# Moving the S5 branch of a two-block network kernel in beside the retention products

## What is computed

```python
def even_mixer(h, pos, w_in, w_out, ...):
    proj = h @ w_in                      # (512, 1024) @ (1024, 2560)
    q, k, v, g, u = jnp.split(proj, [512, 1024, 1536, 2048], axis=-1)
    ret = retention(rotary(heads(q), pos), rotary(heads(k), pos), heads(v))
    ret = head_layer_norm(ret).transpose(0, 2, 1, 3).reshape(bsz, s_len, RET_WIDTH)
    ret = silu(g) * ret
    ssm = s5_mixer(u, ...)
    return jnp.concatenate([ret, ssm], axis=-1) @ w_out

def s5_mixer(u, ...):
    # x_t = a * x_{t-1} + B u_t, complex, 32 groups of 16 channels with 64 states
    _, states = lax.associative_scan(combine, (a, bu), axis=1)
    y = jnp.einsum('gcp,bsgp->bsgc', c_mat, states).real + d_skip * uf
    y = gelu(y)
    return y * sigmoid(y @ w_glu)
```

## Time and profile before

| | |
|---|---|
| median of 3 runs | 3015.39 us (3014.43 to 3018.1) |
| the profiled execution, its own time | 3018.45 us |
| its span | 3016.6 us |
| TensorE busy | 2796.2 us, 93% of the span |
| VectorE busy | 1603.4 us, 53% |
| ScalarE busy | 1150.8 us, 38% |
| mean clock granted to TensorE | 0.954 |
| chain that ended last | 42% TensorE, 6% VectorE, 1% DMA, 1% ScalarE |

### The profile page before, as it was taken

How to read it: one execution, slowest core, us unless ns; L and a number is a source line. 1 busy time by engine, 2 the same in 40 slices (tenths; PEclk the granted TensorE clock), 3 DMA queues, 4 the chain that set the end, 5 groups by cost and what they waited for, 6 DMA issues and landing times.

```text
span 3016.6 us, 33666 instructions
## 1 busy us (share of the span) xinstructions
PE 2796.2 (93%) x12976; PEld 2007.7 (67%) x12976; DVE 1603.4 (53%) x2021; ACT 1150.8 (38%) x1502; POOL 240.3 (8%) x232
## 2 busy tenths in 40 slices
PE   5987899999999999999699879999999978999998
PEld 3855675556655545666377568888877746888886
DVE  5557644566655545665464535444465475434445
ACT  3342313455544534554232234323353265322334
POOL 1064630000000000000100000000000000000000
PEclk8998989999999999999789789999999989999999
DMA  7234739999999989999832123232322201233210
GB/s 232 71 127 135 278 128 396 410 414 416 416 415 412 418 353 359 418 418 419 338 118 85 56 91 92 90 105 91 105 93 74 85 9 42 88 95 105 87 53 28
DMA packets 163338, 615.95 MB, mean 204 GB/s; under 512 B 15349, under 2 KB 33795, under 8 KB 112644
## 3 DMA queue, kind: packets, MB, share of 16 engines
q1 hardware_dynamic: 149232, 571.39, 50.3%
q0 software_dynamic: 9840, 30.78, 3.0%
q10 hardware_dynamic: 4100, 11.59, 1.0%
HBM read 596.88 MB, written 25.43 MB: 206 GB/s over the span
## 4 chain that ended last, share of the span: by engine, by line
PE 42%; DVE 6%; DMA 1%; ACT 1%; issue 1%; DVEq 0%; SPq 0%; POOL 0%; ACTq 0%; POOLq 0%
PE ps L274 41%; DVE arena L194 2%; DVE arena_r L205 1%; ACT arena L239 1%; DMA ring<-row_scratch 1%; DVE H L194 1%; PE ps L290 0%; DVE arena L217 0%; DMA ring<-s_ww 0%; DVE arena L213 0%; DVE H L205 0%; DVE arena L205 0%; ACT wunits L468 0%; DVE ring_r L478 0%; DVE arena L201 0%
## 5 line engine op out<-in xcount | busy, mean ns | idle before, releaser
L274 PE MATMUL ps<-arena_r,wunits 128*128 128x512 f32 (+1 forms) x3552 | 1112.0, 395 | 15.6 <-DVE arena_r L194 7.9
L478 DVE TENSOR_TENSOR ring_r<-ring,wunits 128x1024 fp32r<-128x1024 f32 (+1 forms) x513 | 615.7, 1223 | 648.0 <-ACT wunits L468 634.4
L468 ACT ACTIVATE wunits<-ring 128x1024 fp32r<-128x1024 f32 (+1 forms) x513 | 529.1, 1049 | 733.9 <-PE ps L274 698.7
L274 PEld LDWEIGHTS ps<-arena_r,wunits 128*128 128x128 f32 x3552 | 671.7, 190 | 165.3 <-issue 15.8
L274 PE MATMUL ps<-arena_r,ring_r 128*128 128x512 f32 (+1 forms) x1776 | 695.6, 392 | 0.0
L274 PE MATMUL ps<-wunits,arena_r 128*128 128x512 f32 x1792 | 511.8, 398 | 3.7 <-ACT wunits L468 3.7
L274 PEld LDWEIGHTS ps<-wunits,arena_r 128*128 128x128 f32 x1792 | 334.0, 188 | 89.7 <-ACT wunits L468 11.1
L274 PEld LDWEIGHTS ps<-arena_r,ring_r 128*128 128x128 f32 x1776 | 337.7, 190 | 70.8
L274 PE MATMUL ps<-ring,arena 128*64 128x512 f32 (+1 forms) x1328 | 337.5, 602 | 11.1 <-issue 6.4
L274 PE MATMUL ps<-arena 128*64 128x512 f32 (+10 forms) x1580 | 278.9, 424 | 49.7 <-DVE arena L194 17.0
L274 PEld LDWEIGHTS ps<-arena 128*64 128x64 f32 (+4 forms) x1580 | 151.2, 183 | 158.8 <-issue 96.2
(11 more groups left out here) (178 smaller groups left out, 1821.6 us busy)
## 6 DMA issues: line engine op xcount, KB each, us to landing
ring<-in_w_gu SPq DMA_DIRECT2D x163, 1024.0 KB, 16.3
ring<-in_w_down SPq DMA_DIRECT2D x125, 1024.0 KB, 15.7
arena<-in_w_gu SPq DMA_DIRECT2D x93, 1024.0 KB, 15.6
ring<-in_w_ada SPq DMA_DIRECT2D x48, 512.0 KB, 5.6
ring<-in_ffn_w_gate SPq DMA_DIRECT2D x44, 512.0 KB, 3.7
ring<-in_ffn_w_up SPq DMA_DIRECT2D x44, 512.0 KB, 3.7
ring<-in_ffn_w_down SPq DMA_DIRECT2D x40, 512.0 KB, 3.6
ring<-in_diff_w_qkv SPq DMA_DIRECT2D x24, 512.0 KB, 3.6
```

Source lines behind the costliest of these rows:

```text
L274: ins = self.e.matmul(o, l_, r_, start=start, stop=stop, skip_group_check=True)
L468: q.inc(q.e.activation(h, raw, ACT.Copy), (st.tag, "hi", i))
L478: q.inc(q.e.tensor_tensor(lo, raw, h.bitcast(F32), ALU.subtract), (st.tag, "lo", i))
```

## The change

The product u3 comes first of the five (and its weights first in the stream). Behind it, each engine gets a generator of 16 steps (`s5_chain_pe`, `s5_chain_act`, `s5_chain_dve`) in `slow`, with `pair` set, which runs beside the 16 units of q3, k3, v3 and g3: step 1 to 5 the transposes of u, 6 and 7 the table MG, 8 VI, 12 ZI, 15 and 16 the table GS; on VectorE step 8 the coefficients, 9 and 10 the multiplications, 11 the scan, 13 and 14 the multiplications and the addition to XS, 15 and 16 copies. The local convolution (`local_pe`) and the addition of YN (`scanned_pe`) stand between the links of the heads, each pair's 8 matmuls of either kind apart. The stage of its own and the barriers `ret done` and `s5 done` are gone. VV, VI, ZZ, YN and the split inputs of the glu product now lie in 4 further ring slots (`SPAN`), so the stream `X` has 6 slots instead of 10 until piece 30, and that piece waits for `glu done`. GS is loaded with MG before the products, WW after MG has been read, KK after XS is made, into the place of WW.

```diff
     LENT = [x for x in OLD if x[1] >= ARENA + 10 * SLOT]
-    X = main_stream("x", [x for x in OLD if x not in LENT])
+    SPAN = [x for x in OLD if ARENA + 6 * SLOT <= x[1] < ARENA + 10 * SLOT]
+    X = main_stream("x", [x for x in OLD if x not in LENT and x not in SPAN])
...
             if len(X.pieces) == 30:
-                for x in LENT:
-                    x[3] = ("all", "lent back")
-                X.slots = list(reversed(LENT)) + X.slots
+                for x in LENT + SPAN:
+                    x[3] = ("all", "glu done")
+                X.slots = list(reversed(LENT)) + X.slots + SPAN
...
-    for c in range(5):
+    for c in (4, 0, 1, 2, 3):
         plan_x(l_in, 8, c * 512, 512)
...
     def ret_pe(p):
-        dense_pe(p, X, "q3", [512], hn("mix0"), 8, after=rot_after(p, "q3", lambda c, m: Q3[:, m, :]),
-                 between=first_beside_pe(p))
+        dense_pe(p, X, "u3", [512], hn("mix0"), 8, between=first_beside_pe(p))
+        p.slow, p.pair = [s5_chain_pe(p)], True
+        dense_pe(p, X, "q3", [512], hn("mix0"), 8, after=rot_after(p, "q3", lambda c, m: Q3[:, m, :]))
         dense_pe(p, X, "k3", [512], hn("mix0"), 8, after=rot_after(p, "k3", lambda c, m: K3[:, m, :]))
         dense_pe(p, X, "v3", [512], hn_tm("mix0"), 8, mode="tm")
         dense_pe(p, X, "g3", [512], hn("mix0"), 8)
-        dense_pe(p, X, "u3", [512], hn("mix0"), 8)
-        p.finish_jobs()
+        p.finish_all()
+        p.pair = False
...
         pair_scores_pe(p, 0)
-        turn_u_pe(p, 0)
+        local_pe(p, 0)
         for pr in range(4):
             pair_out_pe(p, pr)
             if pr < 3:
                 pair_scores_pe(p, pr + 1)
             if pr:
                 norm_var_pe(p, pr - 1)
-            back_u_pe(p, pr)
+            if pr < 3:
+                scanned_pe(p, pr)
             norm_mean_pe(p, pr)
-            if pr < 3:
-                turn_u_pe(p, pr + 1)
-        groups_in_pe(p)
+            if pr != 2:
+                local_pe(p, min(pr + 1, 3))
         norm_var_pe(p, 3)
+        scanned_pe(p, 3)
...
+    def s5_chain_pe(p):
+        turn_u_pe(p, 0)
+        yield
         for j in range(4):
+            back_u_pe(p, j)
+            if j < 3:
+                turn_u_pe(p, j + 1)
+            yield
+        for g0 in range(0, 32, 8):
+            groups_in_pe(p, g0)
+            if g0 % 16:
+                yield
...
+            p.mm(PB[b][:, :], jmT, VV[:, g0 * 64:(g0 + 8) * 64], True, True, name)
+        for _ in range(4):
+            yield
+        p.wait_ge(*dve("scanned"))
...
+            p.mm(PB[b][:, :], jmT, ZZ[:, g0 * 512:(g0 + 1) * 512], True, True, ("zi", g0))
+        for _ in range(3):
+            yield
+        for g0 in range(0, 32, 4):
+            out_groups_pe(p, g0)
+            if g0 % 16 == 12:
+                yield
...
+    def s5_chain_dve(v):
+        for _ in range(7):
+            yield
+        v.wait_ge(*pe("vv", 24))
+        v.copy(D0, R8.unsqueeze(2).to_broadcast([128, 32, 64]))
...
+        v.wait_ge(*loaded("s5ww"))
...
+        v.tt(VV, VV, WRf, ALU.mult)
+        yield
+        v.wait_ge(*act("vi", 24))
+        v.tt(VI, VI, WIf, ALU.mult)
+        v.tt(VV, VV, VI, ALU.subtract)
+        yield
+        v.scan(ZZ, a(16384, 2048), VV, "scanned")
+        yield
+        v.fill(XS[:, :, 0:1], 0.0)
+        yield
+        v.wait_ge(*act("zi", 3))
+        v.tt(ZZ, ZZ, WRf, ALU.mult)
+        v.tt(ZI, ZI, WIf, ALU.mult)
+        yield
+        v.tt(XS[:, :, 1:64], Z3[:, :, 0:63], I3[:, :, 0:63], ALU.add, "xs")
...
+    def s5_local_load(g):
+        g.wait_ge(*dve("xs"))
+        load(g, "s5kk", xw(4096, 4096), kk_d)
...
         heads_pe(p)
-        all_wait(p, "ret done")
-        s5_in_pe(p)
-        lend(p)
-        s5_out_pe(p)
-        all_wait(p, "s5 done")
         dense_pe(p, X, "glu", [512], of_parts("ss", sp), 4)
...
-        for i in range(10):
+        for i in range(6):
             fetch(s, X, i)
```

More of the change, by code:

```diff
@@ new lines, in out_groups_pe @@
+    def out_groups_pe(p, g0):
+        p.wait_ge(*dve("xs"))
+        p.wait_ge(*loaded("s5gs"))
+        name = ("y5g", g0)
+        b = p.bank(name)
+        p.claim(name)
+        for g in range(4):
+            p.mm(PB[b][0:64, g * 128:(g + 1) * 128], XS[:, g0 + g, :], GS[:, (g0 + g) * 128:(g0 + g + 1) * 128],
+                 g == 0, g == 3, name if g == 3 else None)
+    def s5_chain_pe(p):
+        turn_u_pe(p, 0)
+        yield
+        for j in range(4):
+            back_u_pe(p, j)
+            if j < 3:
+                turn_u_pe(p, j + 1)
+            yield
+        for g0 in range(0, 32, 8):
+            groups_in_pe(p, g0)
+            if g0 % 16:
+                yield
@@ L3561, in s5_in_act @@
[L3561 to L3567 removed]
+        for _ in range(4):
+            yield
+        p.wait_ge(*dve("scanned"))
+        for g0 in range(4):
+            b = p.bank(("zi", g0))
+            p.claim(("zi", g0))
+            p.mm(PB[b][:, :], jmT, ZZ[:, g0 * 512:(g0 + 1) * 512], True, True, ("zi", g0))
@@ new lines, in s5_chain_pe, with s5_chain_act @@
+        for _ in range(3):
[4 more added lines that the diff above has]
+                yield
+    def s5_chain_act(q):
+        turn_u_act(q, 0)
+        yield
+        for j in range(4):
+            back_u_act(q, j)
+            if j < 3:
+                turn_u_act(q, j + 1)
+            yield
+        for g0 in range(0, 32, 8):
+            s5_copy_act(q, ("vv", g0), VV[:, g0 * 64:(g0 + 8) * 64])
+            if g0 % 16:
+                yield
+        for g0 in range(0, 32, 8):
+            s5_copy_act(q, ("vi", g0), VI[:, g0 * 64:(g0 + 8) * 64])
+        for _ in range(4):
+            yield
+        for g0 in range(4):
+            s5_copy_act(q, ("zi", g0), ZI[:, g0 * 512:(g0 + 1) * 512])
+        for _ in range(3):
+            yield
+        for g0 in range(4, 32, 8):
+            out5(q, g0)
+            if g0 % 16 == 12:
+                yield
@@ new lines, in s5_copy_act @@
+    def s5_copy_act(q, name, to):
+        q.wait_ge(*pe(*name))
+        q.copy(to, bank_of(name)[:, :], name)
+        q.free(name)
+    def s5_chain_dve(v):
+        for _ in range(7):
+            yield
+        v.wait_ge(*pe("vv", 24))
+        v.copy(D0, R8.unsqueeze(2).to_broadcast([128, 32, 64]))
+        v.fill(D0[:, :, 0:1], 0.0)
+        yield
+        v.wait_ge(*loaded("s5ww"))
+        v.wait_ge(*act("vv", 24))
+        v.wait_ge(*pe("vi", 24))
+        v.tt(VV, VV, WRf, ALU.mult)
+        yield
+        v.wait_ge(*act("vi", 24))
+        v.tt(VI, VI, WIf, ALU.mult)
+        v.tt(VV, VV, VI, ALU.subtract)
+        yield
+        v.scan(ZZ, a(16384, 2048), VV, "scanned")
+        yield
+        v.fill(XS[:, :, 0:1], 0.0)
+        yield
+        v.wait_ge(*act("zi", 3))
+        v.tt(ZZ, ZZ, WRf, ALU.mult)
+        v.tt(ZI, ZI, WIf, ALU.mult)
+        yield
+        v.tt(XS[:, :, 1:64], Z3[:, :, 0:63], I3[:, :, 0:63], ALU.add, "xs")
+        yield
+        for g0 in range(0, 32, 8):
+            out5(v, g0)
+            if g0 % 16:
+                yield
@@ L4337, in program_sp @@
         combine_sp(s)
-        for i in range(10, len(X.pieces)):
+        for i in range(6, len(X.pieces)):
             fetch(s, X, i)
```

176 lines of the change are left out of this document (62 added, 114 removed).

## The result

The changed kernel takes 2991.16 us, the median of 4 runs (2987.8 to 2992.15), beside 3016.74 for the kernel before (3014.43 to 3019.08, 4 runs): a ratio of 0.9913 [0.9899, 0.9927]. It is 25.6 us less; the working had 26.1 less. The prediction was 2989, range 2977 to 3002. The profiled execution took 2992.15 us.

A forecast was written before the change was run, and what follows sets the result against it. Idle time and half clock between u3 and glu, 42 us together, were the gain's ceiling; TensorE was already busy in the products. 32.9 added, 61.0 saved, 2 for clock: -26.1, from the 3015.39 median to 2989 us, range 2977 to 3002.

The forecast's parts named there:

- the working: Whole kernel: 32.9 us added, 61.0 less in the heads, 2 for the clock, so 26.1 us less.
- Matmuls among the products: Chain work between product units, priced at full clock: 25.5 us, with MG 7.7, VI and ZI 3.7 each.
- The scan wait: Among the products at step 12: TensorE waits 4.7 us for VectorE's scan, with ZI and g3 queued behind.
- The entry of the heads: Between g3's end and the heads: VectorE begins 5.4 us after, where it was 2.7, so 2.7 later.
- the two waits that I had named: In the heads: TensorE idle 3.2 us before the last mean and 5.6 before the glu product.
- The path to `glu`: From VectorE's entry to the heads until the glu product: 59.7 us by way of ScalarE, 61.0 less than before.
- The clock in the heads: In the heads: half clock in part of the last matmuls costs 2 us, between none and some 5.
- It only moves work: Rival, in the heads: VectorE bounds them, local convolutions find no room, gain only 7 us, 3008; chance 0.07.
- Elsewhere: Outside products and heads: u product equal in length to q3, later FFN weight requests stay hidden; nothing added.
- The ring: Rival, weight stream: 6 slots too few, pieces stop TensorE, 3016 to 3025; this or a like stall elsewhere, chance 0.06.
- the threshold that I gave: Weight stream: landing over 24.6 us stops TensorE; the ring decides the outcome from a landing of 31 us.

The follow-up runs named there:

- e_serial: Changed kernel with all 16 S5 chain steps run one after the other behind g3, not between units: 3022.76 us, ratio 1.0029 to the kernel before.
- e_apart: Changed kernel with the local convolutions and YN additions put behind the heads' last variance: 3001.51 us, ratio 0.9954 to the kernel before.
- r_after: The changed kernel timed again, unchanged, as the measure for the runs beside it: 2989.53 us, ratio 0.991 to the kernel before.
- e_fill: Changed kernel with 18 matmuls that nobody reads put ahead of TensorE's wait for the scan: 2991.39 us, ratio 0.991 to the kernel before.
- e_scan: Changed kernel with VectorE's chain up to the scan one step earlier, TensorE's order unchanged: 2986.48 us, ratio 0.9899 to the kernel before.
- e_local3: Changed kernel with tile 3's local convolution moved ahead of the last mean in the heads: 2989.14 us, ratio 0.9911 to the kernel before.
- e_gelu: Changed kernel with GELU and split of three tiles ahead of the last root, last YN addition ahead of the last variance: 2980.29 us, ratio 0.9879.
- e_ring4: Changed kernel with 4 weight slots in place of 6 until piece 30: 3002.6 us, ratio 0.9954 to the kernel before.
- e_all: Changed kernel with VectorE's chain earlier, GELU early and the last local convolution ahead of the last mean: 2980.23 us, ratio 0.9878.

## Why the prediction was right

The total was met to 2 us, and the mechanism is the one forecast: e_serial and e_apart take its two halves away, and 33 and 12 us of time are lost. That it came out so near is in part luck. Among the products 30.2 us were expected (25.5 and 4.7) and 32.4 came, 2.2 more; in the heads 61.7 were expected (59.7, and 2 for the clock) and 59.05 came, 2.7 less. The two errors have opposite signs. In r_after the second is 1.8 (59.92).

- *Matmuls among the products.* MG came out at 7.36 us for 7.7, VI at 3.60 for 3.7, the output table at 3.71 a half for 3.9. The decision to price MG at full clock, against its own row of 13.11, was right, and e_serial shows that the instruction has both lengths in the new order too: in one piece behind the short waits of the transposes the same 64 records took 13.89, at a clock of 0.50. Between full units MG is also split in two; whether its neighbours or the split keep it at full clock, no run separates.
- *ZI* was mis-sized: 6.55 for 3.7. It follows the wait for the scan, and its window has a clock of 0.56. That 2.9 is more than the whole excess on this side (the others came out some 0.7 below their prices), and e_fill showed it by giving ZI back its 3.70. I had counted the wait and not what it does to the work behind it.
- *The scan wait*, 4.7 expected, was 4.58, by the very rows of the working: multiplication and subtraction, three rotary operations, scan. XS cost nothing. e_scan showed that taking the wait away brings 3.4 us, where the next thing that VectorE owes TensorE, the copy of v3, comes 2.2 us late instead.
- *The entry of the heads* was 5.4 us behind g3's last matmul (1674.49 to 1679.89), as worked out.
- *Inside the heads* the two waits that I had named were there: 3.60 for 3.2 before the last mean, 5.98 for 5.6 before `glu`. e_local3 and e_gelu tell which of the two was worth anything: the first under 1 us, the second some 7 (5.5 ahead of `glu` and 1.4 in it).
- *The path to `glu`.* The working went by ScalarE (root, table load, four GELUs, then 1.6 us): first high part at 58.1 us, measured 57.35, then 1.7. It left out that VectorE's splits stand behind its last normalisation (root, reciprocal of 3.35, two products), which ended at 1738.09, 0.1 us before the first split. ScalarE's first high part ended about 0.2 us ahead of that (2.62 for four, from 1737.24). So two paths ended together, and the number would have been off had VectorE's been longer. `glu` needs nothing of that normalisation, but taking it out of the way alone would have won some 0.2 us; e_gelu moved both.
- *The clock in the heads.* I took 2 us. The profile of the changed kernel shows a clock of 0.98 and next to nothing of it, r_after 1.7 us, of which 0.9 reached the start of `glu`. In the former the two errors of the clock, 2 too many here and 2.9 too few at ZI, nearly cancel. The Trainium skill ("TensorE: Matmul & The Clock Gate", HAM oscillation) says that short gaps do no harm and that a longer one brings half clock. The traces of the changed kernel agree at both ends: full clock behind gaps up to 1.10 us, half clock at first behind 4.54 and more. Between them, at 3.60, the same kernel ran the last local convolution at full clock once (4.18) and in part at half the other time (5.88). That sustained work ends half clock, as the prediction has it from that page, e_serial doesn't bear out at MG: it stayed at a clock of 0.50 for 13.89 us without a gap.
- *It only moves work* fell: the heads took 59 us, not 80. TensorE's new work fitted into its waits, and what I had not counted as a gain of the placing, the clock, is 8.3 of the 14.6 us that e_apart shows.
- *Elsewhere* I took nothing. From the first matmul of `w_out` to the end it is 1233.4 us, and 1231.6 before; the other versions lie between 1229.8 and 1235.2, so a loss of that size can't be told.
- *The ring.* It didn't decide, as forecast, yet the threshold that I gave was wrong. I had TensorE want a piece five units after it is asked for. But ScalarE makes the high part four units ahead of TensorE, so with 6 slots it wants the piece about two units (10.9 us) after it is asked for. The landing of 3.6 us, at most 6.7, was still inside that. With 4 slots it asks for the piece when it already wants it, so each landing is waited for, and the price was 13 to 15 us by way of ScalarE's queue.

## What to carry to other kernels

Price work that is moved between full TensorE units at the clock of its new neighbours, and count the first matmuls behind a wait of 4.5 us or more at half clock, as in all these versions (behind 3.6 us it went either way); filling gaps with needed work pays twice, in idle time and in clock. Of two idle gaps in a row, remove the last one: filling the earlier one only lengthens the later, when both hang on the same engine's order. When a buffer ring is shortened, ask which engine reads a piece first and what stands behind that read in its program, since the delay travels there and not to the consumer of the product.

## What the hardware showed beyond that

- Behind one and the same gap of 3.6 us the clock differs from execution to execution. The last mean and the local convolution behind it took 1.12 and 4.18 us in the first profile of the changed kernel, 1.12 and 5.88 in r_after and in e_ring4, 1.87 and 5.17 in e_gelu, 1.95 and 5.10 in e_serial, 2.08 and 6.03 in e_scan, 2.08 and 6.08 in e_fill. So full clock throughout was the exception, one of seven. As one kernel shows two of these cases, such a difference can't be put down to an edit; what decides it, these runs don't tell. It is worth up to 2.9 us. ZI behind its wait of 4.58 wanders likewise, between 5.19 and 6.75 us.
- Without any edit ahead of it, the stage began at 1517 to 1527 us in the twelve profiles. The length of the stage leaves this out: e_all and e_gelu differ by 3.1 us in the stage and by 0.1 in the medians. But it comes from one execution of each kernel, and its parts wander with the clock by up to 1.7 us in the one kernel that was profiled twice. So a difference of 1 or 2 us in it shows nothing by itself, and one of 3 us wants its own wait or its own rows as a witness.
